# Encoder trunk on one core: the norm's root is taken out of the way to the first projections and put to their sums

## The reference

```python
for l in range(DEPTH):
    h = _rmsnorm(x, attn_norm_w[l])                 # x * rsqrt(mean(x*x) + eps) * w
    (g_qkv, g_z, g_b, g_a, d_q, d_k, d_v, c_q, c_k, c_v, gate_raw) = _split_cols(h @ w_in[l])
    y_a = _gdn_mixer(g_qkv, g_z, g_b, g_a, ...)     # gated delta rule, beta from g_b, decay from g_a
    y_b = _diff_mixer(d_q, d_k, d_v, ...)           # differential attention, rotary on q and k
    y_c = _gqa_mixer(c_q, c_k, c_v, ...)            # grouped queries, RMSNorm of q and k by head, axial rotary
    x = x + merged(y_a, y_b, y_c, gate_raw) @ w_out[l]
    x = x + _hier_moe(_rmsnorm(x, ffn_norm_w[l]), ...)
return _rmsnorm(x, final_norm_w)
```

## Time and profile before

| | |
|---|---|
| runs | 1600.32 us median of 3 (1599.47 to 1601.37) |
| span of the profiled execution, first to last instruction | 1596.4 us |
| the median stands above that span by | 3.9 us; the profiled execution has no other time of its own |
| PE busy | 1304.0 us (82%) |
| DVE busy | 669.7 us (42%) |
| ACT busy | 461.2 us (29%) |
| POOL busy | 120.7 us (8%) |
| bytes read from HBM | 488 MB, 306 GB/s over the span |
| mean granted clock of PE | 0.957 of 2.4 GHz |

### The profile page before, as it was taken

One profiled execution on the slowest core, in us unless ns is written; L12 is line 12 of the kernel. 1 busy time (PEld: TensorE's weight loads), 2 busy tenths in 40 slices (PEclk: granted clock), 3 DMA queues, 4 the chain that ended last, 5 costly groups with the idle time before them and its releaser, 6 DMA issues. The chain is left out here.

```text
span 1596.4 us, 46360 instructions
## 1 busy us (share of the span) xinstructions
PE 1304.0 (82%) x19436; PEld 992.4 (62%) x19437; DVE 669.7 (42%) x1614; ACT 461.2 (29%) x952; POOL 120.7 (8%) x108
## 2 busy tenths in 40 slices
PE   7998899987787777777799989999877776676675
PEld 6887687765555455555578877777555554454443
DVE  6666856662222111111286776766522221111112
ACT  3456645441111000001145565554311110100101
POOL 2002630000000000000020044200000000000000
PEclk9999999999999988889999999999999999999898
DMA  9531025499999999999974310455999999999996
GB/s 342 203 123 54 14 106 190 179 391 384 423 424 429 429 427 427 428 428 427 411 263 159 118 46 3 161 205 211 389 389 402 426 427 426 429 427 428 429 427 289
DMA packets 80202, 490.59 MB, mean 307 GB/s; under 512 B 13262, under 2 KB 15846, under 8 KB 52454
## 3 DMA queue, kind: packets, MB, share of 16 engines
q1 hardware_dynamic: 80102, 489.16, 75.4%
HBM read 488.09 MB, written 1.05 MB: 306 GB/s over the span
## 5 line engine op out<-in xcount | busy, mean ns | idle before, releaser
L2059 PE MATMUL ps<-ring,arena 128*32 128x128 f32 x5632 | 195.4, 297 | 79.1 <-DMA ring<-in_expert_w_gate_dram 69.6
L2059 PEld LDWEIGHTS ps<-ring,arena 128*32 128x32 f32 x5632 | 172.8, 120 | 109.1 <-DMA ring<-in_expert_w_gate_dram 73.7
L2141 ACT ACTIVATE arena<-ps 128x128 f32<-128x128 f32 x66 | 18.3, 277 | 531.0 <-PE ps L2059 531.0
L2290 DVE TENSOR_SCALAR arena<-cst,arena 128x128 f32 x132 | 39.8, 344 | 222.3 <-issue 217.4
L2059 PE MATMUL ps<-arena 128*32 128x128 f32 x2688 | 97.4, 305 | 41.1 <-DMA arena<-in_expert_w_gate_dram 38.7
L2059 PEld LDWEIGHTS ps<-arena 128*32 128x32 f32 x2688 | 86.1, 124 | 55.1 <-DMA arena<-in_expert_w_gate_dram 44.0
L482 POOL TENSOR_TENSOR small<-small,cst 128x8 f32<-128x8 f32 (+1 forms) x21 | 27.7, 1317 | 1219.4 <-DVE small L756 454.0
L1814 DVE TENSOR_TENSOR w_low<-ring,w_high 128x512 fp32r<-128x512 f32 x126 | 85.8, 705 | 51.8 <-ACT w_high L1738 51.8
L2025 PE MATMUL ps<-xn,arena 128*32 128x256 f32 x1088 | 73.7, 388 | 40.5 <-DVE arena L2236 40.4
L2241 DVE COPY arena<-ps 128x256 f32<-128x256 f32 x68 | 28.9, 425 | 178.6 <-PE ps L2025 178.5
L1738 ACT ACTIVATE w_high<-ring 128x512 fp32r<-128x512 f32 x126 | 77.2, 634 | 74.3 <-PE ps L1674 62.0
(11 more groups left out here) (372 smaller groups left out, 2509.5 us busy)
## 6 DMA issues: line engine op xcount, KB each, us to landing
ring<-in_expert_w_up_dram SPq DMA_DIRECT2D x44, 2048.0 KB, 39.4
ring<-in_expert_w_gate_dram SPq DMA_DIRECT2D x42, 2048.0 KB, 40.3
ring<-in_w_in_dram SPq DMA_DIRECT2D x28, 2048.0 KB, 7.9
ring<-in_expert_w_down_dram SPq DMA_DIRECT2D x22, 2048.0 KB, 40.6
ring<-in_expert_w_down_dram SPq DMA_DIRECT2D x44, 1024.0 KB, 39.0
arena<-in_expert_w_up_dram SPq DMA_DIRECT2D x20, 2048.0 KB, 40.5
arena<-in_expert_w_gate_dram SPq DMA_DIRECT2D x20, 2048.0 KB, 40.2
arena<-in_expert_w_down_dram SPq DMA_DIRECT2D x20, 2048.0 KB, 41.4
```

The lines of the kernel that those rows point to most:

```text
L2059: ins = pe.matmul(bank_b[32 * g:32 * g + 32, u * P:(u + 1) * P], xg[:, c], spare[:, c, g] if from_tenth else w[:, u, c, g], start=(c == 0) ...
L2290: v.tensor_scalar(selw[:, t], bcast(cst[:, bass.ds(r * CAP + K_IOTA, CAP)].unsqueeze(1), [P, 4, CAP]), posn[:, t, bass.ds(e, 1)], weight[: ...
```

## The change

- The projections of units 0 to 4 work on h without its root: x turned, times the gain. ACT rounds each 256-token half from PSUM (`high`, with the gain as scale), DVE subtracts from the same bank (`low`), chunk by chunk. The eight chunks of x now lie in six banks and two halves; the last two are turned behind the products of chunks 0 and 1.
- The root multiplies the sums: in ropes (three-operand operations), in the squares (scale), in the copies of the values.
- ACT now takes the squares of both token halves, behind chunks 3 and 5. The root is asked for behind low part 6, spread on PE behind unit 0, and copied by DVE behind low part 10. The two unread matmuls are gone.
- POOL makes the normed `HT` as high + low, times the spread root, in four quarters (`normed`): the first as soon as the spread root is copied, the other three behind the four roots of the ropes. ACT makes `HT_hi` anew in the attention block, behind two heads' exponentials, as two copies of 1024 elements; POOL waits for them ahead of `HT_lo`.
- Beta's and decay's 16 columns are copied by POOL beside the 256 narrow ones of unit 1; its chunks are 272 wide and have eight buffers of their own. The 32 small matmuls are gone.
- In layer 0 unit 0 is loaded in two parts (a quarter, on a semaphore of its own, and the rest); the parameter loads stand ahead of x, the table of -0.5 behind unit 0.
- In layer 1 ACT makes the high parts of chunks 0 and 1, and DVE the low part of chunk 0 and the copy of the columns, ahead of their copies of x. PE turns x quarter by quarter as it is copied.

```diff
@@ load_unit
+        if l == 0 and u == 0:
+            sp.dma_start(dst[:, 0:2], src[:, 0:2]).then_inc(s_first, 16)
+            dst, src = dst[:, 2:KC], src[:, 2:KC]
         sp.dma_start(dst, src).then_inc(landed[u % UNITS], 16)
@@ project_sync
             sp.dma_start(cst[:, 0:P], consts[:, 0:P]).then_inc(s_ident, 16)
-            sp.dma_start(cst[:, K_HALF:K_ALL], consts[:, K_HALF:K_ALL]).then_inc(s_ident, 16)
+            load_early(sp, l)
             sp.dma_start(X, x.rearrange("b (t p) d -> p (b t) d", p=P)).then_inc(s_x, 16)
-            load_early(sp, l)
             load_unit(sp, l, 0)
+            sp.dma_start(cst[:, K_HALF:K_ALL], consts[:, K_HALF:K_ALL]).then_inc(s_half, 16)
@@ project_tensor
-        for n in range(2):
-            pe.matmul(ps[0][:, :], ident, X[:, 0, 0:512], start=True, stop=True)
+            if q < 2:
+                turn_x(6 + q)
             if q == KC - 1:
-                pe.wait_ge(p_early, 16 * 3 * (l + 1))
+                pe.wait_ge(a_root, 1)
                 for t in range(NT):
-                    for cc in range(KC):
-                        ins = pe.matmul(ps[7][:, t * 16:(t + 1) * 16], HT[:, cc, t * P:(t + 1) * P], wba[:, cc],
-                                        start=(cc == 0), stop=(cc == KC - 1))
-                ins.then_inc(b_ba, 1)
+                    ins = pe.matmul(spread[:, t * P:(t + 1) * P], bcast(rstd[:, t:t + 1], [P, P]), ident, start=True, stop=True)
+                ins.then_inc(a_spread, 1)
@@ project_scalar
+        def high(c):
+            act.wait_ge(a_turned, c + 1)
+            act.activation(HT_hi[:, c], a_banks[c], ACT.Copy, scale=g_attn[:, c:c + 1]).then_inc(b_hh, 1)
+        act.wait_ge(a_gain, 1)
         for q, (u, c, cols) in enumerate(chunks_b):
+            if q < KC:
+                high(q)
+            if not (l and q < 2):
+                weights_high(act, l, q)
+            if q == 3:
+                x_ready(act, l)
+                squares_of_x(0)
+            if q == 5:
+                squares_of_x(1)
@@ project_vector
+        def low(c):
+            v.wait_ge(b_hh, c + 1)
+            v.scalar_tensor_tensor(b_HT_lo[:, c], a_banks[c], g_attn[:, c:c + 1],
+                                   HT_hi[:, c].bitcast(F32), ALU.mult, ALU.subtract).then_inc(b_hl, 1)
+            if q == KC - 2:
+                v.wait_ge(a_squares, NT)
+                v.tensor_scalar(rstd, ss, 1.0 / D_MODEL, EPS, ALU.mult, ALU.add).then_inc(a_asked, 1)
+            if q == KC + 2:
+                v.wait_ge(a_spread, 1)
+                v.tensor_copy(spread_sb, spread).then_inc(a_spread_kept, 1)
@@ project_pool
+        pool.tensor_copy(unit8(U_CKV)[:, :, 256:NARROW_W], wba).then_inc(b_wba, 1)
+        def normed(j):
+            part = slice(2 * j, 2 * j + 2)
+            if j == 0:
+                pool.wait_ge(b_hl, KC)
+                pool.wait_ge(a_spread_kept, 1)
+            pool.tensor_tensor(HT[:, part], HT_hi[:, part].bitcast(F32), b_HT_lo[:, part].bitcast(F32), ALU.add).then_inc(a_sum, 1)
+            pool.wait_ge(a_sum, j + 1)
+            pool.tensor_tensor(HT[:, part], HT[:, part], bcast(spread_sb.unsqueeze(1), [P, 2, SEQ]), ALU.mult).then_inc(a_ht, 1)
+        normed(0)
         ...
+        roots(pool, b_asked, b_root, [hrs[:, 0:8], hrs[:, 0:8], hrs[:, 0:2], hrs[:, 0:2]])
+        for j in range(1, 4):
+            normed(j)
@@ ACT, attention block
                 exps(1)
+                for j in range(2):
+                    act.activation(HT_hi[:, 4 * j:4 * j + 4], HT[:, 4 * j:4 * j + 4], ACT.Copy).then_inc(g_hh, 1)
@@ ACT, end of the experts
                 jobs(act, job)
+                if l + 1 < depth:
+                    for q in range(2):
+                        weights_high(act, l + 1, q)
                 act.wait_ge(m_scattered, 1)
@@ DVE, end of the experts
+                if l + 1 < depth:
+                    weights_low(v, 0)
+                    columns_out(v)
                 v.wait_ge(m_scattered, 1)
```

More of the change, by code:

```diff
@@ L290, in encoder_trunk @@
     b_w_hi = rounded("b_w_high", "arena", 13056, 6, 512)
+    b_n_hi = rounded("b_narrow_high", "arena", 8448, KC, NARROW_W)
     w_lo = [rounded(f"w_low{n}", "ring", n * 4096, 4096) for n in range(UNITS)]
@@ L486, in encoder_trunk @@
     s_x, s_ident, s_cst = (top.enter_context(nc.semaphore(n)) for n in ("x_landed", "identity_landed", "constants_landed"))
[L487 to L492, removed]
+    m_x, m_x_dve = sem("m_x_written_act"), sem("m_x_written_vector")
+    s_half = top.enter_context(nc.semaphore("half_landed"))
+    s_first = top.enter_context(nc.semaphore("first_weights_landed"))
+    a_squares, a_asked, a_root, a_spread, a_spread_kept, a_turned, a_convt, a_gain, a_sum, a_ht = (
+        sem("a_" + n) for n in ("squares", "root_asked", "root", "root_spread", "root_spread_kept", "turned", "columns_turned", "gain", "hT_summed", "hT"))
+    a_banks = [bank[:, 0:SEQ] for bank in (*ps[4:8], *ps[2:4])] + [bank[:, SEQ:2 * SEQ] for bank in ps[4:6]]
+    spread, columns_bank = ps[7][:, 0:SEQ], ps[7][:, 0:76]
+    b_hh, b_hl, b_hi, b_lo, b_used, b_wba = (sem("b_" + n) for n in ("hT_high", "hT_low", "w_high", "w_low", "w_used", "beta_columns"))
     b_free, b_rope, b_turned, b_out = sem("b_free"), sem("b_rope"), sem("b_turned"), sem("b_out")
-    b_chain, b_sq, b_ba, b_asked, b_root = sem("b_chain"), sem("b_squares"), sem("b_ba"), sem("b_root_asked"), sem("b_root")
+    b_chain, b_sq, b_asked, b_root = sem("b_chain"), sem("b_squares"), sem("b_root_asked"), sem("b_root")
     streamed_b = (U_CQ, U_CKV, U_DQ, U_DK, U_DV)
@@ L526, in x_ready @@
         else:
-            eng.wait_ge(m_x, 4)
+            eng.wait_ge(m_x, 2)
+            eng.wait_ge(m_x_dve, 2)
     def project_sync(sp, l):
@@ L546, in project_tensor, with turn_x @@
     def project_tensor(pe, l):
-        pe.wait_ge(s_ident, 32)
-        x_ready(pe, l)
-        for c in range(KC):
+        pe.wait_ge(s_ident, 16)
+        pe.wait_ge(p_columns, 16 * 3 * (l + 1))
+        pe.transpose(columns_bank, convrows[0:76], ident[0:76, 0:76]).then_inc(a_convt, 1)
+        if l == 0:
+            pe.wait_ge(s_x, 16)
+        def turn_x(c):
+            if l:
+                pe.wait_ge((m_x, m_x_dve)[c // 2 % 2], c // 4 + 1)
             for t in range(NT):
[L551 to L554, removed]
+                ins = pe.transpose(a_banks[c][:, t * P:(t + 1) * P], X[:, t, c * P:(c + 1) * P], ident)
+            ins.then_inc(a_turned, 1)
+        for c in range(6):
             if c == 3:
[L556 to L561, removed]
-        for n in range(2):
-            pe.matmul(ps[0][:, :], ident, X[:, 0, 0:512], start=True, stop=True)
+                pe.wait_ge(a_gain, 1)
+            if c == 5 and l:
+                pe.wait_ge(m_x_dve, 2)
+            turn_x(c)
         def heads(i):
@@ L601, in project_tensor, with weights_high, weights_low, columns_out @@
         unit_landed(pe, l, U_GQ)
+        pe.wait_ge(a_ht, 4)
         for c in range(KC):
             pe.matmul(ps[6][:, 0:SEQ], unit8(U_GQ)[:, c, 0:DH], HT[:, c], start=(c == 0), stop=(c == KC - 1))
+    def weights_high(act, l, q):
+        u, c, cols = chunks_b[q]
+        if q == 0 and l == 0:
+            act.wait_ge(s_first, 16)
+        elif c == 0 or (q == 2 and l == 0):
+            unit_landed(act, l, u)
+        if q == NARROW:
+            act.wait_ge(b_wba, 1)
+        if held_by(q) is not None:
+            act.wait_ge(b_used, held_by(q) + 1)
+        act.activation(high_b(q), unit8(u)[:, c, 0:cols], ACT.Copy).then_inc(b_hi, 1)
+    def weights_low(v, q):
+        u, c, cols = chunks_b[q]
+        v.wait_ge(b_hi, q + 1)
+        v.tensor_tensor(w_lo[u % UNITS][:, c * 512:c * 512 + cols], unit8(u)[:, c, 0:cols], high_b(q).bitcast(F32),
+                        ALU.subtract).then_inc(b_lo, 1)
+    def columns_out(v):
+        v.wait_ge(a_convt, 1)
+        v.tensor_copy(columns_in, columns_bank).then_inc(a_gain, 1)
     def project_scalar(act, l):
@@ L611, in squares_of @@
             n = 512 if items[i][0] == U_CQ else 128
-            act.activation(squares[:, i % 2, 0:n], ps[i % 4][:, 0:n], ACT.Square).then_inc(b_sq, 1)
+            act.activation(squares[:, i % 2, 0:n], ps[i % 4][:, 0:n], ACT.Square, scale=rstd[:, i % NT:i % NT + 1]).then_inc(b_sq, 1)
         def heads_out(i):
@@ L678, in rope @@
             src = ps[i % 4]
+            root = rstd[:, t:t + 1]
             v.wait_ge(*product_done(i))
@@ L776, in project_vector @@
+        v.wait_ge(a_gain, 1)
         for q, (u, c, cols) in enumerate(chunks_b):
             n = q // KC
-            if q >= 4:
-                w_low(q)
+            if q < KC:
+                low(q)
+            if not (l and q == 0):
+                weights_low(v, q)
+            if q == KC - 2:
[4 more added lines that the diff above has]
+                v.tensor_copy(spread_sb, spread).then_inc(a_spread_kept, 1)
+                v.wait_ge(a_root, 1)
+                v.wait_ge(s_cst, 16)
@@ L800, in project_pool @@
```

(1 more changed line is left out.)

128 lines of the change are left out of this document (33 added, 95 removed).

## The result

| | before | changed |
|---|---|---|
| median of 4 runs, us | 1599.9 | 1617.3 |
| span of the profiled execution, us | 1596.4 | 1614.2 |
| mean granted clock of it | 0.957 | 0.955 |

The ratio of the times is 1.0104, with a 95% interval of 1.0088 to 1.0121. The forecast was 1609.4, with a range up to 1614: the sign was right, 8 us were missing.

The account below looks back on a forecast made before the run. DVE was taken to decide up to rope(0) and chunk 17, with POOL's operations holding it up. Layer 0 +3.0 and layer 1 +6.1 made +9.1 on the 1596.4 span, 1609.4 us from the 1600.3 median; range 1599 to 1614.

Parts of the forecast that it names:

- Clock: Layer 1's start: PE idle about 4 us could bring half clock, up to 1.7 us; only in the range.
- before chunk 16 PE then simply waits: Layer 0: PE time saved on beta and decay is worth nothing beyond the -1.7 and the margin of 0.9.
- Layer 0 up to chunk 17: Layer 0's start: earlier rope(0) -1.7, POOL beside the narrow subtractions +2.0, margin at chunk 17 -0.9.
- -1.7: Layer 0: rope(0) could start at 26.7 against 28.40, before POOL's cost, with loads landing some 0.7 later.
- The added POOL work: Each layer: each normed-h operation on POOL costs DVE 1.0 us; two before rope(0), six before chunk 28.
- 3.4 + 0.2: Each layer: six POOL operations, +6.0 less 2.6 of cover, are +3.4 on PE; small copies and longer ropes +0.2.
- Layer 1's start: Layer 1 up to rope(0): waiting for unit 0's load +0.5, POOL operations +2.0, no margin at chunk 17.
- At nothing: Items costing nothing, among them the attention block's two ACT copies, 2.2 us, covered by ACT's idle 2.33.
- Rival (a): POOL's operations don't hold DVE up: layer 0 -2.4, layer 1 +0.7, 1598.6 us, no difference; chance 0.14.
- Rival (b): PE's queue decides, by the narrow unit's start: -6.6 and -4.4, 1589.3 us; chance 0.08.
- Rival (c): No POOL hold, but layer 1's late unit and 1.7 to 3.4 of half clock: 1602.0, up to 1605.4; chance 0.06.

Follow-up runs that it names:

- the ten places: Chunk 16 in both layers of five kernels (the changed one and four follow-ups) with PE idle 4.67 to 4.89 us ahead of it; no single time.
- the useless work: Changed kernel with 36 unread matmuls ahead of chunk 16 and 18 ahead of chunk 17 on PE, both layers: 1612.1 us, ratio 1.0085.
- the copies first: Changed kernel with layer 1's x copies put back ahead of the first high parts (ACT) and first low part (DVE): 1614.0 us, ratio 1.0090.
- the normed h on the matmul engine: Changed kernel with 16 PE matmuls and eight ACT copies in place of POOL's eight operations, the spread and its copy: 1599.5 us, ratio 0.9994.
- the sum is made twice: Changed kernel with POOL's sum of the two halves made twice in normed(1) to normed(3), both layers: 1619.1 us, ratio 1.0118.
- the ropes split: Changed kernel with DVE's PSUM reads of rope(0) and rope(1) first, the rest of the ropes behind later low parts: 1610.2 us, ratio 1.0065.
- one such swap: Kernel combining PE-made normed h, x copies first and split ropes, with ACT's evacuations moved behind the high parts of chunks 20 and 21: 1592.7 us, ratio 0.9952.

## Why the forecast was right in kind and too small

**The step that failed is Clock: "I leave it out of the sum and in the range"**, with 1.7 once, for layer 1's idle start. Beside it stands "before chunk 16 PE then simply waits", at no price. But the narrow unit starts 7.6 us earlier while chunk 16 still waits for the ropes, and so the change makes idle time on PE, 4.89 us in layer 0 and 4.67 in layer 1, where before 32 matmuls and the narrow unit filled it. From chunk 17 to 22 the profiled execution lost 2.4 and 2.0 us, of which only 0.4 and 0.3 are seen where chunk 17 ran at full clock; late in layer 1 a longer stretch at 0.50 goes with another 3.2. That is 6.9 us by the clock, of the 8.7 that the span lies above the forecast. The wait of DVE didn't hide it, because DVE waits for PE there too: rope(2) stood idle 2.73 until PE had done chunk 17 and the head transposes behind it. As the ten places show, this is what the slow matmuls cost when they last into chunk 17, and not what every execution pays.

**Layer 0 up to chunk 17**: forecast -0.6 (-1.7 + 2.0 - 0.9), measured -1.0, with rope(0) at 28.11 for the 28.7 forecast. That this came out is in part luck. In the five profiles whose layer 0 has the same code up to chunk 17, but for the useless work in one, rope(0) starts at 28.1, 28.2, 29.6, 30.3 and 30.6, and chunk 17 comes at -1.0, -0.9, +0.5, +1.2 and +1.4 against before. In the last three chunk 0 ran with matmuls of 0.63, in the first two it didn't. At chunk 22 the four of them without the useless work lie together again, at +1.35 to +1.84: the half clock took its time either at the start or behind the idle time, and by there the loss is much the same. Of the kernel before there is only one profile, with a fast start, so how much its own start varies isn't known. The reason given for the -1.7 was half right at best: three quarters of what chunk 0 gained came from the loads, which the forecast had at 0.7 later.

**The added POOL work**: forecast 1.0 an operation, measured 1.09; the six cost 4.1 and 4.4 (a further 3.4 us at half clock, 849.94 to 853.35, lies in the latter) for 3.4 + 0.2. The mechanism is shown by three runs: with more such operations, with none, and with the same ones at another place. The two on the five narrow subtractions cost DVE 2.3 (4.22 for the five, with pitches of 1.46 and 1.45 for 0.35), for 2.0 forecast.

**Layer 1's start**: forecast +0.5 and +2.0, and no margin, measured 3.9. ACT's x copies did wait for the ring's DMA, 3.90, and PE's transposes took 2.79. With the copies first 2.2 came back, and the transposes took 1.53. The wait was forecast; the 1.4 above it is near those 1.26 us of slow transposes, for which the 1.7 had been kept out of the sum. No run holds that share alone, so it stays an estimate.

**At nothing**: the attention block's ACT copies. The shift is 5.5 before and after them, so this holds.

**Late in layer 1** 3.2 us are added between 920 and 960 us, where the code is the same. Windows of the changed kernel, and of the one with the normed h on the matmul engine:

```profile
930.00:960.00 30.00, 26.42 (x169) 23.37 (x167) 19.86 (x49) 16.64 (x44) 7.53 (x5) 0.77 0.20 71
```

```profile
930.00:960.00 30.00, 23.64 (x196) 21.09 (x199) 22.39 (x60) 20.34 (x44) 22.04 (x17) 0.94 0.06 7
```

The kernel before has 0.94 there too. In the ten experiments' profiles the stretch from 920 to 985 us adds -0.2 to 0.0 (four of them), 1.3 to 1.6 (four) or 3.2 to 4.1 (two). It goes with the time that the clock spent at 0.50 in that stretch: 3.4 or 6.8 us in the first four (3.4 in the kernel before), 10.2 in each of the next four, 17.1 and 20.5 in the last two, and 17.1 in the changed kernel with its 3.2. So the clock makes the difference; why it is granted in one execution and not in another was not tried and stays open. It was in no forecast, and isn't the work of any edit that I could name.

In sum: 9.1 forecast; +2.5 in layer 0, of which 0.8 is lost again in its experts, +4.2 in layer 1, +3.2 late, -0.4 at the end: 17.8 on the profiled execution.

**Rival (a)** fell with 8.53 for 3.09, and with the positions of chunks 22 to 28 when the sum is made twice. **Rival (b)** fell: chunk 16 waited 4.89; only with the ropes split does PE follow on at once, and then POOL's hold limits the gain. **Rival (c)** had the missing term, 1.7 to 3.4 of half clock, but as an alternative to the hold where both were true.

## What to carry to other kernels

Before crediting an engine with time saved, ask what it does with it: if it only waits longer for another, PE may also lose its clock for the work behind the wait, and that can have a price where the wait has none. Work moved to GpSimd is free beside VectorE only where VectorE reads PSUM or has slack; where a transposed product can make the same tensor on an idle PE, that can be cheaper, as it was here. When one queue is unblocked, look at once at which other queue holds an instruction with a long wait ahead of one that is ready: here one such swap was worth 4.2 us by the medians, 2.6 of them seen in the stage itself. And before a profile is read against a forecast of a few us, profiles of several executions should be laid side by side.

## What the runs showed of the hardware

- Idle for 4.67 to 4.89 us, PE ran the chunk behind it with matmuls of 0.63 at ten of ten places, and the next chunk too at seven; in the changed kernel the clock read 0.50 for 10.24 us both times. Kept busy by 36 and 18 unread matmuls it stayed at 1.00.
- Two executions with the same code up to there ran chunk 0 with matmuls of 0.63 and of 0.40; this moved the narrow unit by 1.5 us, and by up to 2.5 in others. The profile's clock reads 1.00 in both. The Trainium skill (TensorE: Matmul & The Clock Gate, Part 1: The HAM clock gate) says that the same kernel is slow for a different number of matmuls from run to run; the traces agree. A single profile can therefore be off by as much as the effect looked for.
- GpSimd and VectorE operations with two SBUF operands each take turns: 1.69 us from one low part to the next for 0.60, with POOL's own operation going from 1.37 to 1.73.
